# First operand tiles of the next stage split ahead of the last addition to x, state rows turned in other stages: a hybrid decoder step

## The chip, the cores and the metric

The kernel runs on one core of a Trainium2 chip. The metric is the device time of one execution in microseconds (us). TensorE does the matrix products (PE in the profile; PEld is its weight load), VectorE (DVE), ScalarE (ACT) and GpSimd (POOL) work on rows, and DMAs are issued by SyncE (SP) and by ScalarE. PSUM is the memory that TensorE writes, in eight banks of 512 floats for each of 128 partitions.

## The reference

One inference step of a trunk of two layers, for a prompt of 1024 tokens and for 8 single sample tokens with the same weights; D = 1024, F = 2816. Cut to what matters:

```python
for i in range(2):
    h = rmsnorm(x, norm_mix[i])
    # layer 0: pointwise + GLU, causal depthwise conv of width 31, LayerNorm, swish, pointwise (pw2)
    # layer 1: sliding-window attention, 16 heads over 4 kv heads, learned sinks, then w_o
    out = conv_module(h) if i == 0 else attention(h)
    x = x + out
    h = rmsnorm(x, norm_ffn[i])
    g, u = split(h @ ffn_w_in[i])              # 2 x 2816 columns
    x = x + (silu(dwconv3(g)) * u) @ ffn_w_down[i]
y = rmsnorm(x, norm_final)
# also returned: the last 30 rows of the GLU output, the last 128 keys and values,
# and the last two rows of each g, for the prompt and for the samples
```

## The kernel before

All 1032 tokens are the columns of x, which stays on the chip as 8 tiles X of 128 rows. A dense product is three matmuls per weight tile and chunk of 344 columns, since each operand is split into a rounded high part and the rest (weights by GpSimd, lines 577 and 579; operand tiles H by ScalarE, high part, and VectorE, rest). `dense` (line 1717) makes one output tile of 128 rows: 8 operand tiles k, 9 matmuls each, into banks 0 to 2 (side 0) or 3 to 5 (side 1), in turn. A norm's token scale is not applied to H. Only the norm's gain is; the sums of squares are turned into a scale while the next product already runs, and whoever takes the product multiplies by RS, the scale spread over all partitions.

The kernel meets four transitions, where a stage's last output is added to x and x becomes the next stage's operand: after pw2 (into the first ffn), after the first ffn (into qkv), after w_o (into the second ffn), and after the second ffn (into the end). At each of them `residual` runs on two engines. VectorE (line 854) adds a product to its X tile (`x_add`, lines 850 and 852), and sums squares that ScalarE made (`add_square`, line 819). ScalarE (line 1278) squares each X tile (line 1269). After the next-to-last tile, ScalarE waits until the last product is done (`s_mm`), since that product still reads H, and makes the high parts of H tiles 0 and 1 (line 1291); VectorE adds the last tile to x and makes the rest of tiles 0 and 1 (`split_lo`, line 812). Then ScalarE squares the last tile and makes high parts 2 to 7 in a loop (line 1296), and VectorE adds the last squares and makes the rests 2 to 7, in a loop too.

TensorE goes on with `dense(0, 0, wait_h=True, hooks={2: token_sums})`: it waits for each H tile, and after tile 2 it sums the squares over the partitions (`token_sums`, line 1776, 18 matmuls with one column each). ScalarE takes the roots (line 1274), VectorE the reciprocals (line 829), and in the second product, after tiles 1 and 4, TensorE spreads the scale (`broadcast`, line 1783, 16 matmuls; `broadcast_samples`, line 1790, 2). A hook stands in TensorE's instruction order, so a hook that waits holds up everything behind it.

In pw2 and w_o the eight products follow each other with 72 matmuls each. In the ffn, x is added to in passes of 8 groups of 18 matmuls (line 1762), which read MID and not H. The flag `wide` in VectorE's `residual` is for these: there it adds two tiles and then two squares.

Before pw2 stands the layer norm. ScalarE takes a root (line 1406), loads the table for Silu, and per tile makes a Silu and a copy into H (lines 1414 and 1416). TensorE meanwhile spreads scale and mean and then waits for H in `dense_pair` (line 1735).

The end, line 2052 of TensorE's program: `token_sums`; eight transposes of CKEEP (kept GLU rows); 44 of GKEEP (kept gate rows of both ffns, 10 rows per tile) in four parts of 11; then x, by 72 transposes of 128 columns. ScalarE first multiplies X by the last gain (line 1547), takes the roots between, and copies two of the four parts (line 1554); VectorE copies the others (lines 1234 and 1237). The y blocks are scaled by VectorE (even, line 1240) and ScalarE (odd, line 1558) and stored by SP (line 555), the sample row last (line 557). ScalarE's queue issues the six stores of kept rows after its last y block (lines 1561 to 1565). WK is a set of nine work tiles: 0 RS, 1 sum of squares, 2 and 3 squares, 4 to 6 the ffn's, 7 and 8 tables.

Of the kernel before, what the change touches and what calls it, by code (L numbers as in the profile page):

```python
# [126 lines left out]
def build(nc, a):  # L127
    ctx = ExitStack()
    with ctx:
# [135 lines left out]
        s_hh = sem("h_hi_ready")  # L265
        s_h = sem("h_ready")
# [68 lines left out]
        s_ka = sem("gate_rows_taken_by_act")  # L335
# [13 lines left out]
        GROWS = [WK[:, 6:9, :].rearrange("p a n -> p (a n)"), WK[:, 0:3, :].rearrange("p a n -> p (a n)")]  # L349
        HALF_F = F // 2  # L350

        def GATE_PS(part):

            return PS[0:2 + NS, 2 + 3 * part:5 + 3 * part, :].rearrange("p a n -> p (a n)")[:, 0:HALF_F]

        def Y_PS(b):

            pair = 2 * (b % 4)
            return PS[:, pair:pair + 2, :].rearrange("p a n -> p (a n)")
        LNOUT = [WK[:, k, 0:T] for k in (4, 5, 2)]  # L360
# [25 lines left out]
        STORES = 19  # L386
# [5 lines left out]
        def _(sp):  # L392
# [156 lines left out]
            yr.n = 5 + 3  # L549
# [7 lines left out]
            sp.dma_start(a["y_sample"][:, 0, :], WK[0:NS, 4, 0:D]).then_inc(s_st, 16)  # L557

            sp.wait_ge(s_st, 16 * STORES)

# [233 lines left out]
        def _(dve):  # L794
# [59 lines left out]
            def residual(side_of, bias, wide, row):  # L854
# [255 lines left out]
            def ffn(l):  # L1110
                norm_scale()
                base = l * NFR
                v.memset(GB[:, 0:2], 0.0).then_inc(s_v, own.up())
# [39 lines left out]
                with turns(dve, 0, FT // 4, dict([(mm, 24), (pr, 24), (own, 12)] + [(c, 4) for c in (t2, gc, silu, m_, mh, mid)])) as i:  # L1153
                    for o in range(2):
# [5 lines left out]
                        for m in range(1, KT):  # L1160
                            x_add(m, m % 2)
                residual(lambda o: o, None, True, R_MIX + 1 if l == 0 else None)
# [67 lines left out]

            token_scale()
            dve.wait_ge(s_rec, rec.at())
            dve.wait_ge(s_tr, tr.next())
            v.tensor_copy(WK[0:HIST + NS, 5, 0:D], PS[0:HIST + NS, 0:2, :].rearrange("p a n -> p (a n)")).then_inc(s_trr, trr.up())
            for l in range(2):
                dve.wait_ge(s_tr, tr.next(2))
                v.tensor_copy(GROWS[l][0:2 + NS, HALF_F:F], GATE_PS(1)).then_inc(s_trr, trr.up())  # L1237
# [5 lines left out]
            v.tensor_scalar(WK[0:NS, 4, 0:D], PS[0:NS, 0:2, :].rearrange("p a n -> p (a n)"),  # L1243
# [4 lines left out]
        def _(act):  # L1248
# [29 lines left out]
            def residual(row):  # L1278


                acc.n += 1
                with turns(act, 0, KT // 2 - 1, {pr: 2, acc: 2, sq: 2}) as i:
                    for o in range(2):
                        act.wait_ge(s_pr, pr.next())
                        square(tile(X, i * 2 + o), SQ[o])
                act.wait_ge(s_pr, pr.next())
                square(X[:, KT - 2, :], SQ[0])
                if row is not None:
                    act.wait_ge(s_mm, pr.n + 1)
                    for m in range(2):  # L1290
                        F_(H[:, 0, m, :], X[:, m, :], ACT.Identity, scale=par(m, row)).then_inc(s_hh, hh.up())
                act.wait_ge(s_pr, pr.next())
                square(X[:, KT - 1, :], SQ[1])
                if row is not None:
                    with turns(act, 2, KT, {hh: 1}) as m:
                        F_(htile(0, m), tile(X, m), ACT.Identity, scale=par(m, row)).then_inc(s_hh, hh.up())  # L1296
# [109 lines left out]
            F_(TOK[:, 1, :], TOK[:, 0, :], ACT.Sqrt, bias=EPSC[:, :]).then_inc(s_root, root.up())  # L1406
            cen = Count()
# [10 lines left out]
            residual(R_FFN)  # L1418
# [5 lines left out]
            def ffn(l):  # L1424
# [18 lines left out]
                value(0)  # L1443
                gate(1)
                value(1)
# [8 lines left out]
                residual(R_MIX + 1 if l == 0 else None)  # L1454
# [85 lines left out]
            residual(R_FFN + 1)  # L1540
# [3 lines left out]
            xg = Count()  # L1544
            act.wait_ge(s_acc, acc.at())
            for m in range(KT):
                F_(X[:, m, :], X[:, m, :], ACT.Identity, scale=par(m, R_FIN)).then_inc(s_xg, xg.up())  # L1547
                if m == KT // 2:
                    roots()
            turned, taken = 5, 5  # L1550
            ka = Count()
            for l in range(2):
                act.wait_ge(s_tr, turned + 2 + 2 * l)
                F_(GROWS[l][0:2 + NS, 0:HALF_F], GATE_PS(0), ACT.Copy).then_inc(s_ka, ka.up())  # L1554
            act.wait_ge(s_rec, sums.n + 1)
            for b in range(1, NB, 2):
                act.wait_ge(s_tr, turned + 6 + b)
                F_(YOUT[:, b, :], Y_PS(b), ACT.Identity, scale=TOK[:, 2, b:b + 1]).then_inc(s_ya, 1)
            act.wait_ge(s_ka, ka.at())
            act.wait_ge(s_trr, taken + 3)  # L1560
            act.dma_start(a["new_conv_prompt"][0, 0], WK[0:HIST, 5, 0:D]).then_inc(s_st, 16)
# [552 lines left out]
```

## Time and profile before

| | |
|---|---|
| median of 3 runs | 2465.25 us (2464.49 to 2466.59) |
| profiled execution | 2463.03 us |
| its span | 2461.2 us |
| mean granted clock of TensorE | 0.976 of full |
| busy, share of the span | PE 96%, PEld 93%, DVE 50%, POOL 32%, ACT 20% |

Times in the profile are us from the span's start. The line is that of the program printed above. [...] "<-" names what ended a wait.

### The profile page before, as it was taken

What the parts mean: (1) busy time and instruction counts of PE and PEld (TensorE: products, weight loads), DVE (VectorE), ACT (ScalarE), POOL (GpSimd) and SP (SyncE); (2) the same over time, 40 slices, a digit from 0 to 9 for tenths busy, and PEclk for the clock granted to TensorE, in tenths of its full rate; (3) what the DMA queues carried; (4) which work ended last, traced back from release to release, by engine and by line L of the source; (5) the groups of instructions that cost most, each with busy time, mean ns of one, the idle gap of its engine ahead of it and who ended that gap; (6) DMA issues with size and microseconds to landing.
All of it is one profiled execution on the core that took longest, in us unless ns stands there. A gap on an engine that the chain in (4) does not pass through costs nothing. (4 is left out here: it accounts for less than half of the span.)

```text
span 2461.2 us, 36800 instructions
## 1 busy us (share of the span) xinstructions
PE 2355.4 (96%) x15074; PEld 2300.1 (93%) x15074; DVE 1218.4 (50%) x1192; ACT 481.9 (20%) x776; POOL 780.6 (32%) x403
## 2 busy tenths in 40 slices
PE   7999978999999999999989899899999999999996
PEld 6999968899999999999989776889999999999996
DVE  4765565444444443444555698534444434434445
ACT  5111114210011110000120288221111100100014
POOL 2233422233333332333323244222333323323330
PEclk9999989999999999999989899999999999999998
DMA  7322331221211112111112110111121121121112
GB/s 210 74 68 68 83 129 26 60 79 43 52 43 48 46 43 51 43 47 47 43 36 63 23 52 1 35 43 43 44 52 44 43 52 43 44 52 44 51 36 75
DMA packets 175711, 134.09 MB, mean 54 GB/s; under 512 B 11185, under 2 KB 160449, under 8 KB 175263
## 3 DMA queue, kind: packets, MB, share of 16 engines
q1 hardware_dynamic: 168054, 121.78, 18.7%
q10 hardware_dynamic: 7549, 10.71, 1.6%
q8 instruction: 88, 1.44, 0.2%
q14 instruction: 20, 0.16, 0.0%
HBM read 109.42 MB, written 12.32 MB: 49 GB/s over the span
## 5 line engine op out<-in xcount | busy, mean ns | idle before, releaser
L1726 PE MATMUL PS<-H,W 128*128 128x344 f32 x9072 | 1455.9, 322 | 23.7 <-DVE H L812 17.7
L1726 PEld LDWEIGHTS PS<-H,W 128*128 128x128 f32 x9072 | 1444.5, 190 | 27.9 <-issue 17.2
L577 POOL CAST W<-RAW 128x1024 fp32r<-128x1024 f32 x176 | 205.7, 1169 | 1482.0 <-issue 753.4
L1762 PE MATMUL PS<-MID,W 128*128 128x344 f32 x3168 | 503.7, 320 | 1.4 <-DVE X L850 1.4
L1762 PEld LDWEIGHTS PS<-MID,W 128*128 128x128 f32 x3168 | 500.9, 188 | 1.7 <-DVE X L850 1.7
L579 POOL TENSOR_TENSOR W<-RAW,W 128x1024 fp32r<-128x1024 f32 x176 | 479.6, 2725 | 14.1
L850 DVE TENSOR_TENSOR X<-PS,X 128x1032 f32<-128x1032 f32 (+1 forms) x184 | 226.4, 1231 | 248.8 <-PE PS L1762 206.6
L1121 DVE TENSOR_TENSOR WK<-PS,WK 128x1032 f32<-128x1032 f32 x44 | 54.2, 1233 | 310.0 <-PE PS L1726 310.0
L1430 ACT ACTIVATE GKEEP<-WK 128x10 f32 (+1 forms) x44 | 9.3, 212 | 824.4 <-DVE WK L1121 824.4
L1141 DVE TENSOR_TENSOR WK<-PS,WK 128x1032 f32<-128x1032 f32 x44 | 54.2, 1232 | 183.3 <-PE PS L1726 181.0
L1928 PE MATMUL PS<-PB,EB 128*128 128x256 f32 x864 | 108.7, 288 | 13.2 <-issue 6.5
L1124 DVE SCALAR_TENSOR_TENSOR WK<-WK,FPAR 128x1024 f32<-128x1024 f32 x44 | 84.6, 1923 | 73.8 <-ACT WK L1431 73.8
L1928 PEld LDWEIGHTS PS<-PB,EB 128*128 128x128 f32 x864 | 107.5, 196 | 14.0 <-issue 6.7
L1147 DVE TENSOR_TENSOR MID<-WK,MID 128x1032 fp32r<-128x1032 f32 x44 | 88.5, 2010 | 27.3 <-ACT MID L1438 27.3
L1438 ACT ACTIVATE MID<-WK 128x1032 fp32r<-128x1032 f32 x44 | 47.1, 1070 | 246.4 <-DVE WK L1143 246.4
L624 POOL TENSOR_TENSOR PX<-PX,SMALL 128x1024 f32<-128x1024 f32 x32 | 60.6, 1894 | 103.1 <-DVE SMALL L688 103.1
L1433 ACT ACTIVATE WK<-WK 128x1032 f32<-128x1032 f32 x44 | 46.9, 1067 | 189.5 <-DVE WK L1132 189.5
L1269 ACT ACTIVATE WK<-X 128x1032 f32 (+1 forms) x32 | 34.1, 1066 | 192.8 <-DVE X L850 132.4
L819 DVE TENSOR_TENSOR WK<-WK 128x1032 f32<-128x1032 f32 x32 | 58.4, 1825 | 20.8 <-ACT WK L1269 20.5
L1639 PE MATMUL PS<-PT,VR 128*128 128x512 f32 x192 | 59.1, 427 | 2.7 <-ACT PT L1509 2.4
L1126 DVE SCALAR_TENSOR_TENSOR WK<-WK,FPAR 128x1024 f32<-128x1024 f32 x44 | 56.5, 1284 | 5.9 <-DVE WK L1124 0.2
L1501 ACT ACTIVATE PX<-PS,SMALL 128x256 f32<-128x256 f32 x128 | 58.7, 478 | 1.0 <-DVE SMALL L681 1.0
(213 smaller groups left out, 1495.8 us busy)
## 6 DMA issues: line engine op xcount, KB each, us to landing
RAW<-in_ffn_w_in SPq DMA_DIRECT2D x176, 256.0 KB, 3.8
RAW<-in_ffn_w_down SPq DMA_DIRECT2D x88, 256.0 KB, 3.7
RAW<-in_conv_w_pw SPq DMA_DIRECT2D x48, 256.0 KB, 4.1
PB<-GS SPq DMA_DIRECT2D x128, 64.0 KB, 2.0
RAW<-in_attn_w_qkv SPq DMA_DIRECT2D x24, 256.0 KB, 3.8
x_spill<-X SPq DMA_DIRECT2D x1, 4128.0 KB, 12.5
X<-x_spill SPq DMA_DIRECT2D x1, 4128.0 KB, 14.7
XIN<-in_x_prompt SPq DMA_DIRECT2D x8, 512.0 KB, 8.8
```

The costliest lines, as they stand in the source:

```text
L577: nc.gpsimd.tensor_copy(W[:, slot, 0, :], RAW[:, slot, :]).then_inc(s_hi, hi.up())
L579: nc.gpsimd.tensor_tensor(W[:, slot, 1, :], RAW[:, slot, :], W[:, slot, 0, :].bitcast(F32), ALU.subtract).then_inc(s_w, ready.up())
L624: nc.gpsimd.tensor_tensor(PX[:, b], PX[:, b], SMALL[:, b, 6, :].unsqueeze(2).broadcast_to((P, GROUP, 2 * P)), ALU.mult).then_inc(s_pn, 1)
L819: v.tensor_tensor(ACC, ACC, SQ[o], ALU.add).then_inc(s_acc, acc.up())
L850: v.tensor_tensor(x, side(s), x, ALU.add).then_inc(s_pr, pr.up())
L1124: v.scalar_tensor_tensor(t, GB[:, 1:1 + SEQ], fpar(f, base + FR_W + 1), t, ALU.mult, ALU.add).then_inc(s_v, own.up())
L1147: v.tensor_tensor(MID[:, q, 1, :], MM, MID[:, q, 0, :].bitcast(F32), ALU.subtract).then_inc(s_mid, mid.up())
L1501: F_(PX[:, b, g, :], PS[:, 2 * b + g // 2, (g % 2) * 256:(g % 2 + 1) * 256], ACT.Exp, scale=SCALE, bias=SMALL[:, b, 1, g:g + 1], accum_out ...
L1639: last = matmul(PS[:, 6 + b, :], vb[:, vp, :], PT[:, pp, s, :], start=(s == 0 and q == 0), stop=(s == 1 and q == 2))
L1726: last = matmul(PS[:, 3 * side + c, 0:CH], W[:, slot, wp, k * P:(k + 1) * P], H[:, hp, k, c * CH:(c + 1) * CH], start=(k == 0 and q == 0), ...
L1762: last = matmul(PS[:, 3 * side + c, 0:CH], W[:, slot, wp, t * BANK + m * P:t * BANK + (m + 1) * P], MID[:, first + t, hp, c * CH:(c + 1) * ...
L1928: last = matmul(PS[:, 6 + g % 2, (g // 2) * SPP:(g // 2 + 1) * SPP], EB[:, g % 2, wp, NPH * (NLAG - 1 - j):NPH * (NLAG - j), :].rearrange( ...
```

## The change

**Transitions.** FIRST = 3. VectorE makes the rests of H tiles 0 to 2 before the last `x_add`, the rests 3 to 7 after it, then the last squares; the loop is written out. ScalarE makes high parts 0 to 2 before the square of the next-to-last tile (after an ffn), or after it and after a new signal `s_hf` (after pw2 and w_o): TensorE gives it when the last product of the stage is through with operand tiles 0 to 2. High parts 3 to 6 follow when the last product is done, part 7 when the last x is there, and then its square. `token_sums` moves from tile 2 to tile 6 of the first product, the two broadcasts from 1 and 4 to 2 and 5 of the second.

**Kept rows.** CKEEP is turned before `dense_pair`, into banks 4 and 5; ScalarE copies it between its root and its first Silu; TensorE waits for that copy; SP stores it ahead of the later pw2 loads. The first ffn's gate rows are turned in the second ffn, in three parts, in the third and fourth product; ScalarE copies them after `value(0)` and `gate(1)` and issues their stores.

**End.** ScalarE multiplies each X tile by the last gain right after its square, with the table for the root loaded ahead. TensorE turns the second ffn's 22 gate tiles before `token_sums`; ScalarE copies 12, VectorE 10 of them; SP stores them ahead of y. The y blocks follow at once.

```diff
@@ SP
+            sp.wait_ge(s_ckt, 1)
+            sp.dma_start(a["new_conv_prompt"][0, 0], CROWS[0:HIST]).then_inc(s_cks, 16)
+            sp.dma_start(a["new_conv_sample"][0, :, HIST - 1, :], CROWS[HIST:HIST + NS]).then_inc(s_cks, 16)
...
+            sp.wait_ge(s_gkt, 4)
+            sp.wait_ge(s_gku, 1)
+            sp.dma_start(a["new_ffn_prompt"][1, 0], GROWS[1][0:2, 0:F]).then_inc(s_st, 16)
+            sp.dma_start(a["new_ffn_sample"][1, :, 1, :], GROWS[1][2:2 + NS, 0:F]).then_inc(s_st, 16)
@@ VectorE, residual
+                if row is not None:
+                    for m in range(FIRST):
+                        split_lo(m, X[:, m, :], par(m, row))
                 one(KT - 1)
                 if row is not None:
-                    for m in range(2):
+                    for m in range(FIRST, KT):
                         split_lo(m, X[:, m, :], par(m, row))
                 if wide:
                     add_square(0)
                 add_square(1)
                 acc_marks.append(acc.n)
-                if row is not None:
-                    with turns(dve, 2, KT, {hh: 1, h: 1}) as m:
-                        split_lo(m, tile(X, m), par(m, row))
@@ ScalarE, residual
+                if gain is not None:
+                    F_(TOK[:, 3, 0:1], EPSC[:, :], ACT.Sqrt)
...
                         square(tile(X, i * 2 + o), SQ[o])
+                        if gain is not None:
+                            gained(i * 2 + o, gain)
...
+                if row is not None and freed is None:
+                    first_sides(0, FIRST)
                 act.wait_ge(s_pr, pr.next())
                 square(X[:, KT - 2, :], SQ[0])
...
+                if freed is not None:
+                    act.wait_ge(s_hf, freed)
+                    first_sides(0, FIRST)
+                    act.wait_ge(s_mm, pr.n + 1)
                 if row is not None:
+                    first_sides(FIRST, KT - 1)
                 act.wait_ge(s_pr, pr.next())
+                if row is not None:
+                    first_sides(KT - 1, KT)
                 square(X[:, KT - 1, :], SQ[1])
@@ ScalarE, layer norm and second ffn
             F_(TOK[:, 1, :], TOK[:, 0, :], ACT.Sqrt, bias=EPSC[:, :]).then_inc(s_root, root.up())
+            act.wait_ge(s_ck, 1)
+            F_(CROWS, PS[0:HIST + NS, 4:6, :].rearrange("p a n -> p (a n)"), ACT.Copy).then_inc(s_ckt, 1)
...
                 gate(0)
                 value(0)
+                if l == 1:
+                    take_gate_rows(0)
+                    take_gate_rows(1)
                 gate(1)
+                if l == 1:
+                    take_gate_rows(2)
+                    act.wait_ge(s_gkt, 3)
+                    act.dma_start(a["new_ffn_prompt"][0, 0], GROWS[0][0:2, 0:F]).then_inc(s_gks, 16)
+                    act.dma_start(a["new_ffn_sample"][0, :, 1, :], GROWS[0][2:2 + NS, 0:F]).then_inc(s_gks, 16)
                 value(1)
@@ TensorE
+                    if free and k == FIRST - 1:
+                        last.then_inc(s_hf, 1)
...
+            for m in range(KT):
+                last = transpose(PS[0:HIST + NS, 4 + m // 4, (m % 4) * P:(m % 4 + 1) * P], CKEEP[:, m, :])
+            last.then_inc(s_ck, 1)
+            pe.wait_ge(s_ckt, 1)
             dense_pair()
...
+            def gate_rows(part):
+
+                if part == 0:
+                    pe.wait_ge(s_bcr, bcr.at())
+                else:
+                    pe.wait_ge(s_gkt, part)
+                for j, f in enumerate(range(8 * part, min(8 * part + 8, FT))):
+                    last = transpose(PS[0:2 + NS, 6 + j // 4, (j % 4) * P:(j % 4 + 1) * P], GKEEP[:, 0, f, :])
+                last.then_inc(s_gk, 1)
...
-                dense(0, 0, wait_h=True, hooks={2: token_sums})
-                dense(1, 1, hooks={1: broadcast, 4: broadcast_samples})
-                dense(0, 0)
-                dense(1, 1)
+                dense(0, 0, wait_h=True, hooks={6: token_sums})
+                dense(1, 1, hooks={2: broadcast, 5: broadcast_samples})
+                dense(0, 0, hooks=hooks[0])
+                dense(1, 1, hooks=hooks[1])
...
+            ffn(({1: lambda: gate_rows(0), 6: lambda: gate_rows(1)}, {3: lambda: gate_rows(2)}))
```

## Rows read from the trace of the kernel before

**Rows 1.** The page, parts 1 and 2: TensorE busy, granted clock in tenths
```profile
PE 2355.4 (96%) x15074; PEld 2300.1 (93%) x15074; DVE 1218.4 (50%) x1192; ACT 481.9 (20%) x776; POOL 780.6 (32%) x403
...
PEclk9999989999999999999989899999999999999998
```

**Rows 2.** Waits of TensorE, the whole span: total us, times, longest us
```profile
PE PS L1726 <- DVE H L812: 17.7, 6, 3.3
```

**Rows 3.** Windows: us, busy us of PE, PEld, DVE, ACT, POOL, PEclk, DMA
```profile
471.20:504.40 33.20, 27.17 (x154) 26.65 (x153) 16.46 (x12) 11.13 (x12) 8.04 (x4) 0.85 0.34 121
...
1238.00:1272.40 34.40, 28.71 (x153) 28.20 (x153) 18.35 (x14) 11.36 (x14) 7.87 (x4) 0.80 0.12 31
...
1652.60:1685.70 33.10, 27.10 (x155) 26.56 (x154) 16.44 (x12) 11.14 (x12) 8.03 (x4) 0.85 0.13 33
...
2421.60:2461.20 39.60, 19.12 (x142) 16.36 (x142) 14.67 (x12) 18.80 (x19) 0.00 (x0) 0.80 0.33 117
```

**Rows 4.** Timeline, first transition: start us, us, engine, line, work, [idle before]
```profile
473.89 3.06 PE L1726 MATMUL PS<-H,W 128*128 128x344 f32 x18 [2.68 <-DVE H L812]
...
474.31 6.38 ACT L1296 ACTIVATE H<-X,PAR  x6
...
476.86 9.41 DVE L812 SCALAR_TENSOR_TENSOR H<-X,PAR,H  x6
...
480.30 2.95 PE L1726 MATMUL PS<-H,W 128*128 128x344 f32 x9 [3.35 <-DVE H L812]
...
483.04 3.53 PE L1776 MATMUL PS<-CST,WK 128*128 128x1 f32 x18
...
504.14 0.38 PE L1790 MATMUL PS<-CST,TOK 8*128 8x8 f32 x2
```

**Rows 5.** Timelines: TensorE's prices at the full granted clock
```profile
2375.97 45.61 PE L1762 MATMUL PS<-MID,W 128*128 128x344 f32 x288
...
346.21 1.97 PE L1962 MATMUL PS<-CST,WK 128*128 128x1 f32 x18
...
497.99 1.95 PE L1783 MATMUL PS<-CST,TOK 128*128 128x128 f32 x16
```

**Rows 6.** Timeline, second transition: VectorE and GpSimd at the same time
```profile
1241.64 5.41 DVE L819 TENSOR_TENSOR WK<-WK 128x1032 f32<-128x1032 f32 x2
...
1242.70 3.25 POOL L579 TENSOR_TENSOR W<-RAW,W 128x1024 fp32r<-128x1024 f32 x1
```

**Rows 7.** Timeline, before pw2 (340 to 420): the layer norm's start
```profile
359.92 1.28 ACT L1414 ACT_TABLE_LOAD   x1
...
366.04 0.59 PE L1790 MATMUL PS<-CST,TOK 8*128 8x8 f32 x2 [1.32 <-DVE WK L840]
...
368.14 2.26 ACT L1414 ACTIVATE WK<-CONV,PAR 128x1032 f32<-128x1032 f32 x1 [6.94 <-DVE CONV L1091]
```

**Rows 8.** Timeline, the end (2370 to 2461)
```profile
2425.36 5.34 ACT L1547 ACTIVATE X<-X,PAR 128x1032 f32<-128x1032 f32 x5 [1.41 <-DVE WK L819]
...
2429.01 1.89 PE L1796 MATMUL PS<-CST,CKEEP 128*38 128x128 f32 x8
...
2430.72 1.28 ACT L1274 ACT_TABLE_LOAD   x1
...
2432.01 0.27 ACT L1274 ACTIVATE TOK<-PS,EPSC 128x8 f32<-128x8 f32 x1
...
2436.83 2.57 PE L1796 MATMUL PS<-CST,GKEEP 128*10 128x128 f32 x22 [2.94 <-ACT WK L1554]
...
2443.23 1.11 ACT L1558 ACTIVATE YOUT<-PS,TOK 128x1024 f32<-128x1024 f32 x1 [3.67 <-PE PS L1796]
...
2443.61 8.31 SPq L555 DMA_DIRECT2D out_y_prompt<-YOUT  x8
...
2451.96 1.56 SPq L557 DMA_DIRECT2D out_y_sample<-WK  x1
...
2453.96 1.48 ACTq L1565 DMA_DIRECT2D out_new_ffn_sample<-WK  x1
```

More of the change, by code:

```diff
@@ L348, in build @@
         acc_marks = []
[L349 to L354, printed above, removed]
+        GROWS = [WK[:, r:r + 3, :].rearrange("p a n -> p (a n)") for r in (1, 4)]
+        CROWS = WK[0:HIST + NS, 6, 0:D]
         def Y_PS(b):
@@ L1228, in _ @@
             ffn(1)
+            dve.wait_ge(s_gk, 5)
+            v.tensor_copy(GROWS[1][0:2 + NS, 12 * P:16 * P], PS[0:2 + NS, 7, :])
+            v.tensor_copy(GROWS[1][0:2 + NS, 16 * P:F], PS[0:2 + NS, 3:5, :].rearrange("p a n -> p (a n)")[:, 0:F - 16 * P]).then_inc(s_gku, 1)
             token_scale()
             dve.wait_ge(s_rec, rec.at())
[L1233 to L1237, printed above, removed]
             for b in range(0, NB, 2):
@@ L1715, in begin_group, with dense @@
                 pr.n += 1
-            def dense(side, slot, wait_h=False, hooks={}):
+            def dense(side, slot, wait_h=False, hooks={}, free=False):
                 pe.wait_ge(s_w, w.next())
@@ L2009, in _ @@
             ffn()
-            dense(0, 0, wait_h=True, hooks={2: token_sums})
-            dense(1, 1, hooks={1: broadcast, 4: broadcast_samples})
+            dense(0, 0, wait_h=True, hooks={6: token_sums})
+            dense(1, 1, hooks={2: broadcast, 5: broadcast_samples})
             dense(0, 0)
@@ L2047, in _ @@
                 dense(0, 0)
-                dense(1, 1)
-            ffn()
-            token_sums()
-            pe.wait_ge(s_pr, pr.at())
-            for m in range(KT):
-                last = transpose(PS[0:HIST + NS, m // 4, (m % 4) * P:(m % 4 + 1) * P], CKEEP[:, m, :])
-            last.then_inc(s_tr, tr.up())
-            trr.n += 1
-            for l in range(2):
-                for part in range(2):
-                    if l == 1 and part == 0:
-                        pe.wait_ge(s_ka, 1)
-                    if l == 1 and part == 1:
-                        pe.wait_ge(s_trr, trr.next())
-                    if l == 0 and part == 1:
-                        pe.wait_ge(s_root, sums.n + 1)
-                    for f in range(FT // 2):
-                        last = transpose(GATE_PS(part)[:, f * P:(f + 1) * P], GKEEP[:, l, part * FT // 2 + f, :])
-                    last.then_inc(s_tr, tr.up())
-            trr.n += 1
+                dense(1, 1, free=True)
+            ffn(({1: lambda: gate_rows(0), 6: lambda: gate_rows(1)}, {3: lambda: gate_rows(2)}))
+            pe.wait_ge(s_pr, pr.at(1))
+            for f in range(FT):
+                if f == 16:
+                    pe.wait_ge(s_pr, pr.at())
+                bank = 7 if 12 <= f < 16 else f // 4 if f < 12 else f // 4 - 1
+                last = transpose(PS[0:2 + NS, bank, (f % 4) * P:(f % 4 + 1) * P], GKEEP[:, 1, f, :])
+                if f == 11:
+                    last.then_inc(s_gk, 1)
+            last.then_inc(s_gk, 1)
+            token_sums()
             pe.wait_ge(s_xg, KT)
-            pe.wait_ge(s_ka, 2)
-            pe.wait_ge(s_trr, trr.at())
+            pe.wait_ge(s_gkt, 4)
             for b in range(NB):
+                if b == 1:
+                    pe.wait_ge(s_gku, 1)
+                if b == 3:
+                    pe.wait_ge(s_root, sums.n + 1)
                 if b >= 4 and b % 2 == 0:
```

83 lines of the change are left out of this document (47 added, 36 removed).

## The prediction

> **What bounds the kernel now.** I read the page first: TensorE is busy for 96% of the span, and its granted clock is full except in a few slices [rows 1]. So only time in which TensorE stands still or runs at half clock can be won, and it must be looked for in the dips. The waits of TensorE name one: six waits for the rest of an H tile, 17.7 us [rows 2]. That is three transitions with two waits each. The windows measure these transitions, from the end of a stage's last product to the end of `broadcast_samples` in the next one, and the end of the kernel [rows 3]. Each transition takes 33 to 34 us at a mean clock of 0.80 to 0.85; the end takes 39.6 us.
>
> The timeline shows where that goes in the first one [rows 4]: TensorE waits 2.68 us, does 18 matmuls of H tiles 0 and 1, waits 3.35 us because the rest of tile 2 stands behind the last addition, two rests and a square on VectorE, and then works at half clock: 9 matmuls take 2.95 us where a pass at full clock takes 45.61 us for 288, 0.158 each [rows 5]; `token_sums` takes 3.53 us where 18 such matmuls took 1.97 [rows 4, 5].
>
> **First and third transition (after pw2, after w_o).** The work in such a stretch is 117 dense matmuls (18 + 9 + 63 + 27), `token_sums` and the broadcasts. At full clock that is 117 x 0.158 = 18.5, plus 1.97, 1.95 and 0.38 [rows 4, 5]: 22.8 us. The stretches take 33.2 and 33.1 [rows 3], so 10.4 and 10.3 us are lost, 6.0 of each as waits and the rest to the clock. In the changed kernel three tiles are ready before the last product ends: `s_hf` comes with 45 matmuls (7.1 us) to go, and three high parts of 1.06 (6.38 for six [rows 4]) and one rest behind them end in about 4.6. TensorE then has 27 matmuls, 4.3 us, without a wait. In that time VectorE makes the last addition and the rest of tile 3. A rest costs about 1.25: six took 9.41 [rows 4], of which some 2 are a wait behind GpSimd. That wait is visible where two adds of VectorE took 5.41 us with a subtraction of GpSimd, 3.25, lying in them [rows 6]. GpSimd's pair starts with the first product of the stage, so it will meet the rests 3 to 7 now. VectorE needs 1.25 for the addition, 6 x 1.25 for five rests and a square, and 2.2 for the subtraction it meets, 11.0 us; TensorE reaches `token_sums` after 63 matmuls, 10.0 us. One wait of 1.0 us stays, and what is late next is that last square. **Gain: 9.4 and 9.3.** Bounds: 10.4 without any wait, 7.5 if GpSimd costs 2.9 instead of 2.2 and tile 4 is late too.
>
> **Second transition (after the first ffn).** It loses 34.4 - 22.8 = 11.6 us. Here all rests and squares crowd on VectorE: eight rests, the last addition and two squares, 11 x 1.25 = 13.8, plus 2.2 for GpSimd, less the one operation by which the first rest precedes the end of the last group: 14.7. TensorE's 63 matmuls take 10.0; 4.7 us of waits stay, in pieces of 2 or less. **Gain: 6.9.** Bounds: 11 and 2; at the lower one the clock falls as before, which costs 0.20 x 34.4 = 6.9 at most [rows 3].
>
> **End.** Now the last square is added at 2425.36, eight gains of 1.07 (5.34 for five) follow with a table load of 1.28 and the roots in their midst, then the kept rows, and the first y store is issued at 2443.61 [rows 8]. In the changed kernel a gain stands behind each square. Two squares and two gains (4.3) fit into two groups (36 x 0.158 = 5.7), but the last square waits for one gain: the sum is there at 2426.4. The 22 gate transposes (2.57) lie before that, under the squares. `token_sums` at 1.97 gives 2428.4 (3.53 at half clock is the other bound), roots and reciprocal 0.7; meanwhile eight transposes of y (2.57 x 8/22 = 0.9), then a scaling of about 1.2 (1.11 on ScalarE): first store at 2430.6. SP is moved two stores ahead of it, 1.5 each after the copies at about 2427.9, so it is free at 2430.9, and the two bounds meet. Eight issues of 8.31 and the sample's 1.56 end at 2440.6 [rows 8]. The landing of the sample row is not shown; from the last issue's end (2453.96 + 1.48) to the span's end lie 5.8 us, for rows nearly three times as long, so it is between 0 and 5.8, and I take 4. End at 2444.6: **gain 16.6.** Bounds: 18.5 (landing 2) and 12.5 (landing 5.8, sums at half clock, less one).
>
> **CKEEP before pw2.** The last broadcast ends at 366.63; eight transposes take 1.89, ScalarE's copy 1.11, and a table load 1.28 [rows 7, 8]. The load for Silu stood right behind the root, at 359.92, and was hidden in ScalarE's wait of 6.94 us [rows 7]; in program order the copy is now between, and the load follows the copy. The first Silu begins at 371.0 instead of 368.14. Silu and copy, 2.26 + 1.06 per tile, are more than TensorE's 18 matmuls (2.84), so ScalarE is the chain there and nothing takes the delay back. **Cost: 2.9.** Bounds: 0 (the load ahead of the copy after all, which would then lie in the old wait) and 3.5; less than nothing is excluded, as ScalarE's order only gains work. TensorE's own 1.89 lies in its wait for H. SP's wait for the copy delays no weight: the next pw2 loads need a RAW slot that frees only when `dense_pair` lets go of its weights.
>
> [...]
>
> **First ffn's gate rows in the second ffn.** 22 transposes on the bound engine, 2.57, that the end no longer pays but whose saving is already in its gain. The second part waits for ScalarE's copy of the first, behind `value(0)`: 0 to 1.1 (one copy [rows 8]), taken 0.4. **Cost: 3.0.** The copies and two store issues on ScalarE stand before `value(1)`, whose input needs the fourth product (72 matmuls, 11.4 us): hidden.
>
> **At nothing:** the broadcasts one tile later leave two tiles of product (2.8 us) for copying RS and taking the first product off side 0, two operations at 1.25; GpSimd starts its splits as early as the products that trigger them; the unrolled loops are the same operations.
>
> **Sum.** 9.4 + 9.3 + 6.9 + 16.6 - 2.9 - 3.0 = 36.3 us. The profiled execution took 2463.03, its span 2461.2; so 2426.7. The median of the runs shown, 2465.25, is 2.2 above it: **2429**.
>
> **Rivals.**
> *The clock falls again* in the second transition, where 4.7 us of waits lie within 15 us, and at the end, where TensorE has only transposes for 2.6 of 4.8 us. For: the full clock was lost in every transition [rows 3]. Against: in the first transition the clock stood through a wait of 2.68 (18 matmuls in 3.06 behind it) and fell at one of 3.35 [rows 4], while the new ones are 2 or less. Price 6.9 + 2: 2438. Chance 0.15.
> *The change doesn't do what it says:* ScalarE meets `s_hf` too late, because it stands behind the square of the next-to-last tile, and VectorE's rests come after the last addition as before. Then 2.68 comes back in the first and third transition: 2434. Against: 45 matmuls are left after the signal. Chance 0.08.
> *Slower:* the granted clock stays at half after a transition. Its place is the dense run behind the hooks, in which gate rows and broadcasts now break up the products; each us at half clock loses 0.5, so from 73 us of added half clock on, the gain is gone, and at 93 us the time is 2475. Against: before, 0.15 x 33.2 x 2 = 10 us at half clock in a transition, and then full clock on an unbroken run [rows 1, 3]. Chance 0.07, of which 0.03 for a length that lands within 0.2%.
>
> **Numbers.** The forecast has 0.70; its own range is 2421 (no CKEEP cost, landing 2, no late square) to 2434. With the falling clock and the late signal the range is 2421 to 2440. Faster by over 0.2% (5 us, about what a measurement can tell from no change): 0.70 + 0.15 + 0.08 = 0.93; same 0.03; slower 0.04.
>
> **What would show it.** Right: the six waits [rows 2] gone but for about 1 us twice and some 4.7 in the second transition; the stretches [rows 3] at clock 1.0 and near 24, 24 and 28 us; the first y store issued some 9 us behind the end of the last product, where it was 22 (2443.61 against 2421.6); a Silu table load behind a copy, and the first Silu 2.9 later. Wrong: a clock below 0.9 in two of the stretches, a wait for ScalarE's gate rows of more than 2 us, or a span that ends more than 26 us behind the last product.

## The result, and the profile after

The changed kernel takes **2435.62 us** (median of four runs, 2429.5 to 2437.24) against 2464.87 (four runs, 2461.21 to 2466.59): a ratio of **0.9879, 95% interval 0.9865 to 0.9892**. The forecast was 2429 in a range of 2421 to 2440. The profiled execution took 2434.49, its span is 2432.7, so 28.5 us less than the span of before, where the steps of the prediction add up to 36.3. The mechanism came out; 7.8 us of the gain did not come.

The page of the changed kernel, parts 1 and 2 (it answers to [rows 1]):

```profile
PE 2347.4 (96%) x15074; PEld 2290.4 (94%) x15074; DVE 1212.2 (50%) x1191; ACT 484.2 (20%) x780; POOL 782.5 (32%) x403
...
PEclk9999978999999999999999999999999999999999
```

The slices in which the granted clock dipped in the middle and at the end are at 90% or more now. One dip is left, a little deeper than before: the layer norm before pw2, in the sixth and seventh slices.

The windows of the changed kernel over the three transitions and the end (it answers to [rows 3]; columns: us, busy us of PE, PEld, DVE, ACT, POOL, then PEclk, DMA share, GB/s):

```profile
475.30:500.20 24.90, 24.40 (x163) 23.56 (x162) 12.04 (x9) 8.01 (x9) 7.83 (x4) 1.00 0.38 133
1238.50:1268.40 29.90, 26.45 (x164) 25.36 (x163) 16.32 (x14) 8.61 (x11) 8.09 (x4) 0.94 0.14 36
1647.10:1672.00 24.90, 24.38 (x163) 23.54 (x161) 12.05 (x9) 8.01 (x9) 7.83 (x4) 1.00 0.17 43
2410.20:2432.70 22.50, 14.26 (x114) 13.02 (x112) 11.68 (x11) 10.23 (x11) 0.00 (x0) 0.86 0.51 194
```

Each transition runs again from the end of a stage's last product to the end of `broadcast_samples`. That point now lies nine dense matmuls later in the program, 9 x 0.158 = 1.4 us, so the like-for-like lengths are 23.5, 28.5 and 23.5 against 33.2, 34.4 and 33.1. The clock is 1.00 in two of them and 0.94 in the one that keeps its waits; in e2 the first one has the same waits, 0.27 and 0.26 us, and 36 matmuls behind them take 7.46 us for 5.92, so the waits alone don't decide this (see why the prediction was right).

The timeline of the first transition in the changed kernel (it answers to [rows 4]; columns: start us, us, engine, line, work, and in brackets the idle time before and what ended it):

```profile
468.21 3.27 ACT L1307 ACTIVATE H<-X,PAR 128x1032 fp32r<-128x1032 f32 x3 [1.86 <-PE PS L1766]
469.41 3.70 DVE L825 SCALAR_TENSOR_TENSOR H<-X,PAR,H 128x1032 fp32r<-128x1032 f32 x3 [0.54 <-ACT H L1307]
...
475.33 1.29 DVE L865 SCALAR_TENSOR_TENSOR X<-PS,PAR,X 128x1032 f32<-128x1032 f32 x1 [2.21 <-PE PS L1766]
476.54 8.25 DVE L825 SCALAR_TENSOR_TENSOR H<-X,PAR,H 128x1032 fp32r<-128x1032 f32 x5
...
481.23 4.51 PE L1766 MATMUL PS<-H,W 128*128 128x344 f32 x27 [0.26 <-DVE H L825]
...
484.72 1.22 DVE L832 TENSOR_TENSOR WK<-WK 128x1032 f32<-128x1032 f32 x1
485.99 2.07 PE L1818 MATMUL PS<-CST,WK 128*128 128x1 f32 x18 [0.24 <-DVE WK L832]
```

Three tiles are split by 473.1, before VectorE makes the last addition at 475.33; TensorE goes from one stage into the next and waits 0.26 and 0.24 us in place of 2.68 and 3.35. The five other rests run in a row, 1.65 each with GpSimd's subtraction among them, and the last square ends at 485.94, the moment that TensorE wants it.

The timeline of the end in the changed kernel (it answers to [rows 8]):

```profile
2410.27 2.57 PE L1838 MATMUL PS<-CST,GKEEP 128*10 128x128 f32 x22
...
2413.23 1.23 DVE L832 TENSOR_TENSOR WK<-WK 128x1032 f32<-128x1032 f32 x1 [0.39 <-ACT WK L1284]
...
2414.52 2.23 PE L1818 MATMUL PS<-CST,WK 128*128 128x1 f32 x18 [1.69 <-DVE WK L832]
...
2420.07 7.99 SPq L566 DMA_DIRECT2D out_y_prompt<-YOUT  x8
...
2428.11 1.10 SPq L568 DMA_DIRECT2D out_y_sample<-WK  x1
```

The first y store is issued 9.9 us behind the end of the last product (2410.2), where it was 22; the gate rows turn under the last squares. The last issue ends at 2429.2, 3.5 us ahead of the span's end.

What the prediction does not have stands in the queues of the page (part 3: packets, MB, share of 16 engines) and in TensorE's timeline of the first ffn. The queue of instructions in the kernel before:

```profile
q8 instruction: 88, 1.44, 0.2%
```

TensorE's timeline there, at a turn of its loop:

```profile
781.59 22.92 PE L1762 MATMUL PS<-MID,W 128*128 128x344 f32 x144
804.35 45.60 PE L1726 MATMUL PS<-H,W 128*128 128x344 f32 x288
849.78 22.89 PE L1762 MATMUL PS<-MID,W 128*128 128x344 f32 x144
```

The queue of instructions in the changed kernel:

```profile
q8 instruction: 124, 2.03, 0.3%
```

and TensorE's timeline at the same turn:

```profile
777.49 22.91 PE L1804 MATMUL PS<-MID,W 128*128 128x344 f32 x144
801.66 45.72 PE L1766 MATMUL PS<-H,W 128*128 128x344 f32 x288 [1.27 <-DVE X L863]
847.23 22.89 PE L1804 MATMUL PS<-MID,W 128*128 128x344 f32 x144
```

Before, the products went on without a gap; now TensorE stands for 1.25 to 1.30 us at each of four turns (663.74, 801.66, 939.57, 1077.49), at one of them with no releaser but "issue", at the three others with an addition of VectorE for one, which at the same turns of before was never late. From the first to the last down product of the first ffn it is 667.2 us where it was 661.0. And 36 more packets of instructions are loaded, nine for each turn.

| step | predicted us | profiled execution |
|---|---|---|
| first, second, third transition | -9.4, -6.9, -9.3 | -9.7, -5.9, -9.6 |
| end | -16.6 | -17.1 |
| CKEEP ahead of the first Silu (square root to Silu) | +2.9 | +1.4 (8.54 to 9.91) |
| start of pw2's second group | - | -1.3 (the clock, 63 matmuls in 10 us for 55; see the last section) |
| gate rows in the second ffn | +3.0 | +3.2 |
| turns of the loop, first and second ffn | 0 | +6.2, +0.8 |
| layer norm's sums (square root at 363.71, was 359.60) | 0 | +4.1 |
| sum | -36.3 | -27.9 (span: -28.5) |

The right column sets one execution of each kernel against the other, and steps that the change does not touch differ by several us between kernels with the same code there (below).

### The profile page after: what moved, and what is told of

It reads as the page before. It is cut to its first block and busy times, and to the rows that moved or that the text cites. A ratio compares the mean times of both kernels' runs of the same rounds, so it can differ in the third digit from the quotient of the medians.

```text
span 2432.7 us, 36641 instructions
## 1 busy us (share of the span) xinstructions
PE 2347.4 (96%) x15074; PEld 2290.4 (94%) x15074; DVE 1212.2 (50%) x1191; ACT 484.2 (20%) x780; POOL 782.5 (32%) x403
```

## The experiments

All were compared with the kernel before on the same chip. Whether TensorE's turns have to do with where its code lies was asked first.

**The kernel before with its TensorE program moved by four instructions** (e1), and **the changed kernel with two SP loops written out** (e2; the first of the two is shown).

```diff
+            for _ in range(8):
+                pe.wait_ge(s_const, 16)
             pe.wait_ge(s_const, 16)
```
```diff
-            with turns(sp, 2, KT // 2, {ready: 2}) as i:
+            for i in range(2, KT // 2):
```

> The kernel before, with eight waits on a constant that is long there put ahead of TensorE's first instruction, where TensorE waits 11.7 us for x anyway; in the program that is four 64-byte instructions, so that TensorE's loop of the first ffn lies four instructions further on, as it does in the changed kernel (its last instruction goes from place 5630 to 5634; 16 KB are 256 instructions, and 22 x 256 = 5632). Theory (place of the code): the loop now reaches into an eighth block of 16 KB, its instructions are fetched again in every turn, and the four turns of the first ffn each lose 1.2 to 1.5 us that before did not: first ffn 5 to 6 us longer, the queue of instructions over 100 packets instead of 88, total 2469 to 2472 against 2464.9. Rival (the waits at the turns come from the new order of the transitions, or from additions that come later): nothing changes, 2465 within 2, the turns of the first ffn without a wait.

Measured: 2466.23 against 2464.38, ratio 1.0009 (1.0000 to 1.0019); 88 packets, no wait at a turn, 661.0 us. The page counts 36804 instructions for 36800. The rival's numbers.

> The changed kernel, with two of SP's loops of loads (last stage of the convolution block, and q of the attention) written out: the same DMAs in the same order, but four instructions fewer ahead of TensorE's first-ffn loop, which ends at place 5630 again as in the kernel before. Theory (place of the code): the four waits of 1.25 to 1.30 us at the turns of the first ffn (663.7, 801.7, 939.6, 1077.5) go, the first ffn is 5 to 6 us shorter, the queue of instructions back near 88 packets, total 2429 to 2431 against the changed kernel's 2435.6. Rival (the transitions' new timing makes them): waits stay, total 2435 within 3. The clock in the layer norm's sums decides another 0 to 6 us in either: read it from the stage apart.

Measured: 2436.73 against 2464.38, ratio 0.9890 (0.9875 to 0.9905); 124 packets, waits of 1.23 to 1.42 us at all four turns. Again the rival's numbers. But the two runs tell less than was meant, as both expectations have the change's shift of the loop wrong. Counted in the trace's records of TensorE, the turns of a loop once, the loop of the first ffn begins at 3767 in the kernel before, at 3771 in e1, and at 3783 in e2 as in the changed kernel. So e2 moved nothing, and e1 moved the loop by a quarter of what the change moves it: the change has exactly the 16 instructions of the eight CKEEP transposes more ahead of the loop (a weight load and a matmul each). The theory stood, with its place miscounted, and needed a proper test.

**The same padding with 16 instructions** (e5), on the kernel before:

> The kernel before with 32 waits on a constant that is long there ahead of TensorE's first instruction: 16 instructions in the program. Counted without the branch labels, which the first two runs suggest are not in the loaded program, TensorE's first-ffn loop begins at instruction 3800 in the kernels that did not fetch it again (before, the transitions alone; 3804 with the short padding) and at 3816 or 3817 in the three that did (the changed kernel, the SP loops written out, the conv rows late). Here it begins at 3816, with nothing of the change in it. Theory (place of the code): 120 to 125 packets of instructions instead of 88, all four turns of the first ffn wait 1.2 to 1.4 us, the stretch from its first to its last down product is 667 instead of 661.0, total 2470 to 2472. Rival (something of the change itself makes TensorE wait at the turns): 88 packets, 661.0, 2464 to 2467.

Measured: **2472.66** against 2464.82, ratio 1.0038 (1.0026 to 1.0051). The queue of instructions in this kernel, which has nothing of the change but the shift:

```profile
q8 instruction: 124, 2.03, 0.3%
```

and TensorE's timeline at the turn of before:

```profile
785.52 22.91 PE L1762 MATMUL PS<-MID,W 128*128 128x344 f32 x144
809.56 45.70 PE L1726 MATMUL PS<-H,W 128*128 128x344 f32 x288 [1.13 <-issue]
855.10 22.89 PE L1762 MATMUL PS<-MID,W 128*128 128x344 f32 x144
```

Waits of 1.10 to 1.45 at all four turns, 667.0 us; the page counts 36816 instructions for 36800. The place of the code alone makes the loss; the new order of the transitions is not needed for it. The loop of the first ffn begins at 3800 or 3804 in the five kernels with 88 packets and at 3816 or 3817 in the six with 124; the twelfth is the next one. These are counts in the compiled program; those of TensorE's records in the traces are 33 less in every kernel (3767, 3771, 3783, 3784; of e7 and e8, within 2), so the distances are the same.

**Both loops put where they fit** (e6): the conv rows late (below), the first gate-row copy ahead of `value(0)` (TensorE's wait for it is 0.69 us in the changed kernel), and fillers, one instruction between two products, 236 of them in the first groups of pw1 and pw2 and 104 in q. With them the loops of the two ffns begin 3 and 4 instructions ahead of the place that the first has in the kernel before, whole packets of 256 instructions (last section) left out:

```diff
+                            pad()
...
+            def pad():
+                if pads[0] > 0:
+                    pads[0] -= 1
+                    pe.wait_ge(s_const, 16)
+                    pe.wait_ge(s_const, 16)
```

> [...] Theory (place of the code): no wait at any of the eight turns; first ffn 661.0 instead of 667.2, second 660.5 to 661 instead of 664; with the wait of 0.69 about 10 us less than the 2435.4 of the conv rows late: 2425 to 2427, packets of instructions about 55. [...] Rival 2 (the second ffn's turns wait for something else): its stretch stays at 663 to 664, total 2429 to 2430.

Measured: **2423.29** (2422.08 to 2428.11), ratio **0.9841 (0.9828 to 0.9855)**: 12.3 us under the changed kernel, and the fastest version of this study. Its queue of instructions:

```profile
q8 instruction: 53, 0.87, 0.2%
```

and TensorE's timeline at one turn of the first and one of the second ffn:

```profile
772.51 22.92 PE L1816 MATMUL PS<-MID,W 128*128 128x344 f32 x144
795.27 45.60 PE L1767 MATMUL PS<-H,W 128*128 128x344 f32 x288
...
1941.84 22.92 PE L1816 MATMUL PS<-MID,W 128*128 128x344 f32 x144
1964.60 45.60 PE L1767 MATMUL PS<-H,W 128*128 128x344 f32 x288
```

No wait at any of the eight turns: the first ffn 661.0 again, the second 659.3, where before had 663.3 and the changed kernel 664.1. The second loop had been loaded anew in every turn in the kernel before too, unseen, at 0.69 to 0.77 us each, as here:

```profile
1987.48 45.72 PE L1726 MATMUL PS<-H,W 128*128 128x344 f32 x288 [0.77 <-issue]
```

The 340 fillers cost nothing that shows: from the `broadcast_samples` ahead of pw2 to the first down product, with 140 of them between, it is 202.7 us in e6 and in e4, and from the one of qkv to the second ffn's first down product, with the 104 of q between, 477.3 us for 480.9.

**The transitions alone**, on the kernel before (e3; the diff is the change's, without the state rows and the end):

> The kernel before with the three transitions of the change alone (first three operand tiles split ahead of the last addition, the release of the first tiles, token sums after the seventh tile's products, broadcasts one tile later); state rows and the end as before. By the prediction's terms: 9.4 + 6.9 + 9.3 = 25.6 less, 2439; by what the changed kernel's profile showed for them, 9.8 + 6.0 + 9.6 = 25.4. TensorE's first-ffn loop ends at place 5618 here, so by the theory of the code's place nothing is lost at its turns: 2439 to 2440. Rival (the turns' waits come from the transitions): 6 us of it given back, 2445 to 2446. The layer norm's sums: if their half clock in the changed kernel's profile was chance, they stand here as before (square root of the variances at 359.6 within 1) as often as not.

Measured: 2442.69 (2437.16 to 2445.11) against 2464.38, ratio 0.9904 (0.9891 to 0.9918): 21.7 less. 88 packets, 661.0 in the first ffn: nothing lost at its turns, as the place of the code has it. The gain is some 4 us short of the terms; in this profile, which is of the slowest of the five runs, the second ffn's turns took 1.0 more than before, the end 2.3 more (41.9 for 39.6), and the 45 us around the first transition were at a clock of 0.96.

Which half of it brings the gain, the split ahead or the order on TensorE? **The changed kernel with the early order** (e7), **the order alone** (e9) and **the split alone** (e10), the last two on the kernel before:

```diff
-                dense(0, 0, wait_h=True, hooks={2: token_sums})
-                dense(1, 1, hooks={1: broadcast, 4: broadcast_samples})
+                dense(0, 0, wait_h=True, hooks={6: token_sums})
+                dense(1, 1, hooks={2: broadcast, 5: broadcast_samples})
```
(e9 is this, twice; e7 is its reverse on the changed kernel; e10 is e3 without it.)

> The changed kernel with the token sums after the third tile's products again and the broadcasts after the second and the fifth, as in the kernel before, the split ahead kept. Theory of the prediction (the sums behind the products hide the last square): TensorE now stands after 27 products for the last square, which ends at 485.9 in the changed kernel's profile while the 27 products end near 480.5: a wait of 4.5 to 5.5 us in the first and the third transition, 5 to 6 in the second, with a clock that may fall behind it for another 0 to 5 us each; 14 to 20 us in all, 2450 to 2456. Rival (with the split ahead, the splits of the later tiles hold TensorE anyway, so that the wait only moves): under 4 us in all, 2436 to 2439.

Measured: 2456.16 (2444.71 to 2460.73), ratio 0.9959 (0.9938 to 0.9980), 20.5 over the changed kernel: the prediction's mechanism, at the upper end. TensorE's timeline in the first transition:

```profile
483.06 3.70 PE L1818 MATMUL PS<-CST,WK 128*128 128x1 f32 x18 [6.43 <-DVE WK L832]
486.69 12.54 PE L1766 MATMUL PS<-H,W 128*128 128x344 f32 x63
```

One wait of 6.43 us for the last square (8.93 in the second transition), longer than expected, and the clock falls behind it: the sums at 3.70 instead of 2.07, 63 matmuls in 12.54 instead of 10.0.

> The kernel before with the order on TensorE alone changed (token sums behind the seventh tile's products, broadcasts one tile later), the splits where they were. Theory A (from the early hooks in the changed kernel, which cost 20 us: nearly all of the transitions' gain is the order on TensorE, and the split ahead only feeds it): in the first transition the splits of tiles 3 to 8 end at 486.3 in the profile of before, so seven tiles of products end near 486.2, where the changed kernel has 486.0, with waits for tiles of 2.7 and 3.4 us in pieces: 2443 to 2447, within 4 of the 2442.7 of both together. Theory B (both are needed, as the prediction's terms have it: the first tiles' late split takes 2 to 4 us of each transition and the clock falls in those waits): 2450 to 2458.

Measured: 2460.23 against 2463.16, ratio 0.9987 (0.9979 to 0.9996). Theory A, formed from e7, falls; B had 2450 or more and is nearer, but too kind as well.

> The kernel before with the splits ahead and the early release alone, token sums after the third tile's products and the broadcasts after the second and fifth, as before. Theory A (the order on TensorE carries the gain): TensorE stands for the last square after 27 products as before, only longer in one piece (6.4, 8.9 and 6.4 us in the changed kernel with early hooks, against 17.7 in all before): 2460 to 2467, no gain that can be told from none. Theory B (each half brings its share): 2452 to 2458.

Measured: 2465.08 against 2463.16, ratio 1.0005 (0.9996 to 1.0014): no gain, as A had it for this half, and no loss that can be told from none. TensorE's waits over the whole span (total us, times, longest), of e9:

```profile
PE PS L1726 <- DVE H L812: 19.2, 6, 4.5
```

and of e10:

```profile
PE PS L1787 <- DVE WK L821: 25.6, 4, 8.9
```

The kernel before waited 17.7 us for tiles [rows 2]. With the order alone TensorE waits for the same tiles, 19.2; with the split alone it has the tiles and waits for the sums' last square, 25.6 (the fourth wait is the end's). Each half alone trades one wait for another and keeps the fall of the clock (0.90 in the three stretches of e9, 0.77 to 0.82 in those of e10, 0.80 to 0.85 before); both together take 21.7 us. They don't add: a gain of 2.9 and no gain make no 21.7.

**The first tiles released late** (e8):

```diff
-                    act.wait_ge(s_hf, freed)
-                    first_sides(0, FIRST)
                     act.wait_ge(s_mm, pr.n + 1)
+                    first_sides(0, FIRST)
```

> The changed kernel with the first operand tiles released only by the end of the last product of pw2 and of w_o, as before, instead of after that group's third tile; DVE's order (three splits ahead of the last addition) kept. Theory of the prediction (the early release carries the first splits under the last products): ScalarE begins the first side at the products' end, DVE splits three tiles (3.7 us and a first side of 1.07 ahead) before it adds the last tile, the last addition and with it square and sums come 4 to 5 us later, in two transitions: 8 to 11 us, 2444 to 2447. Rival (the first splits are hidden by what follows, the last square sets the end in either): under 3 us, 2435 to 2439.

Measured: 2440.56 (2435.84 to 2448.99), ratio 0.9909 (0.9887 to 0.9930): 4.9 over the changed kernel, between the two expectations, but its four runs lie 13 us apart. The stretches themselves tell more. TensorE waits for H tiles again, in the first transition 2.67 and then 0.60 us, in the third 2.66 and 1.66, and the sums come late:

```profile
473.91 5.87 PE L1765 MATMUL PS<-H,W 128*128 128x344 f32 x27 [2.67 <-DVE H L825]
...
486.35 2.07 PE L1817 MATMUL PS<-CST,WK 128*128 128x1 f32 x18
...
1661.95 2.07 PE L1817 MATMUL PS<-CST,WK 128*128 128x1 f32 x18
```

The last products end at 471.2 and 1646.9, so the sums begin 15.1 us behind them in both, where it is 10.7 in the changed kernel: 4.4 later each, the theory's 4 to 5. VectorE adds the last tile at 476.87, behind three rests. To the end of `broadcast_samples` the two stretches take 29.4 and 30.9 us for 24.9 and 24.9, at a granted clock of 0.94 for 1.00: 10.5 us in all, inside the expected 8 to 11. That the profiled executions, 2440.52 and 2434.49, differ by 6.0 only is due to other stages; the square root ahead of pw2 alone came 4.2 us earlier (359.54 for 363.71). The 5.4 at which the prediction had put a late `s_hf` is the first wait, twice 2.7, and too little.

**The conv rows late** (e4):

```diff
-            F_(CROWS, PS[0:HIST + NS, 4:6, :].rearrange("p a n -> p (a n)"), ACT.Copy).then_inc(s_ckt, 1)
...
             h.n = 2 * KT
+            act.wait_ge(s_ck, 1)
+            F_(CROWS, PS[0:HIST + NS, 6:8, :].rearrange("p a n -> p (a n)"), ACT.Copy).then_inc(s_ckt, 1)
```

> The changed kernel with the convolution rows turned into banks 6 and 7 behind the broadcast, and copied and stored by ScalarE behind the layer norm's last tile in place of ahead of its first Silu; the place of TensorE's loop stays past the border (5635). Theory (the copy and the table load behind it stand on the path of the layer norm): the stretch from the square root to the first Silu goes from 9.91 back to 8.5 to 8.6, total 1.3 to 1.5 less than the changed kernel (2434), the turns of the first ffn still at 1.25 to 1.30. Rival (the transposes or the copy make the next stage's start late wherever they are): the stretch keeps 1 us or the second pair of products of the next stage starts later by as much.

Measured: 2435.39, ratio 0.9884 (0.9869 to 0.9899): the stretch from the root to the Silu goes to 8.34 (10.18 in e2, 9.91 in the changed kernel), and the total does not move by more than the runs differ. The transposes go to banks 6 and 7 here and the two stores to ScalarE, which the diff leaves out. Where the 1.8 us went, the windows of the 10 us from the start of pw2's second group show, in e2 (copy ahead of the Silu):

```profile
403.80:413.80 10.00, 9.91 (x63) 9.92 (x64) 4.19 (x3) 1.07 (x1) 3.66 (x2) 1.00 0.44 107
```

and in e4:

```profile
402.40:412.40 10.00, 9.92 (x53) 9.93 (x54) 4.17 (x3) 1.06 (x1) 3.65 (x2) 0.83 0.42 107
```

e4 begins the group 1.4 us earlier, at a clock of 0.83, and does ten matmuls fewer in 10 us, which is 1.6 us. Neither theory had that.

## Why the prediction was right, and where it was wrong

**Transitions: right in mechanism; the size (25.2 for 25.6) is in part luck.** The waits left are 0.26 and 0.24 in the first, 0.27 and 0.25 in the third, where 1.0 each was predicted, and 0.36, 0.31 (of the weight load), 1.66 and 1.39 in the second, 3.7 where 4.7 was predicted "in pieces of 2 or less". The late last square was named as what is late next, and in the second transition it is (1.39 for `token_sums`). In the second transition the clock is 0.94, between the forecast and the rival in which it falls: 5.9 for 6.9. The argument against that rival was that the clock stands through waits of 2 or less. The 36 matmuls behind `token_sums` show that it need not; the first line is of the first transition of the changed kernel, the next three of its second, the last of the first transition of e2:

```profile
487.99 5.92 PE L1766 MATMUL PS<-H,W 128*128 128x344 f32 x36
...
1245.32 5.91 PE L1766 MATMUL PS<-H,W 128*128 128x344 f32 x36 [1.66 <-DVE H L825]
...
1252.63 2.07 PE L1818 MATMUL PS<-CST,WK 128*128 128x1 f32 x18 [1.39 <-DVE WK L832]
...
1254.63 7.46 PE L1766 MATMUL PS<-H,W 128*128 128x344 f32 x36
...
485.05 7.46 PE L1766 MATMUL PS<-H,W 128*128 128x344 f32 x36
```

In e2, e3, e4 and e6 the first transition has waits of 0.25 to 0.27, as here, and yet these 36 take 7.28 to 7.48 us, some 1.5 more than in the changed kernel; why the clock falls in one execution and not in the other is open. The prediction treated split and order as one step; e9 and e10 show that this was necessary, as no part of it can be priced by itself. The two together, without the rest of the change, measured 21.7 (e3).

**End: right** (17.1 for 16.6). The sums took 2.23, nearer to the full clock's price than to the half clock's 3.53, and the first store came 9.9 behind the last product for the 9 predicted. The landing, taken as 4, was 3.5. Of the "two bounds" that were said to meet, one was misread: the two stores ahead of y were issued in 0.26 and 0.27 us and not 1.5 each, so SP was free long before, and the scaling of the first block (done at 2420.04) set the start.

**CKEEP: the mechanism right, the size wrong.** The table load moved behind the copy, as predicted:

```profile
363.71 0.30 ACT L1439 ACTIVATE TOK<-TOK,EPSC 128x9 f32<-128x9 f32 x1 [11.99 <-DVE TOK L1087]
...
370.21 1.05 PE L1838 MATMUL PS<-CST,CKEEP 128*38 128x128 f32 x8
...
371.30 1.02 ACT L1441 ACTIVATE WK<-PS 38x1024 f32<-38x1024 f32 x1 [7.28 <-PE PS L1838]
372.33 1.28 ACT L1449 ACT_TABLE_LOAD   x1
...
373.62 2.25 ACT L1449 ACTIVATE WK<-CONV,PAR 128x1032 f32<-128x1032 f32 x1
```

The term that was mis-sized is the eight transposes: 1.89 in [rows 8] was a price at half clock (granted 0.50 there), 1.05 is what they took. That is 0.8 of the 1.5 us that were missing; another 0.5 is the last broadcast, which ended 6.6 behind the root where it was 7.0, at a higher clock and not by the change. Against e4, whose broadcasts took what those of e2 took, the copy's cost in this stretch is 1.8 (10.18 for 8.34). And the step "nothing takes the delay back" failed: behind it pw2's second group ran at the full clock, which gave 1.6 of that back (e4).

In the same rows the load starts at the copy's end and the Silu at the load's, 372.33 + 1.28.

**Gate rows: right** (3.2 for 3.0): 1.04, 1.04 and 0.82 for the transposes, each overlapping the next product by some 0.2, and one wait of 0.69 for ScalarE's copy, inside the bounds of 0 to 1.1. e6 took that wait away by placing the copy ahead of `value(0)`.

**The step that failed is "At nothing: ... the unrolled loops are the same operations".** It counts operations, and no term has the place of TensorE's code. The 16 instructions of the CKEEP transposes, whose own time does lie in TensorE's wait for H, push the loop of the first ffn, 1768 instructions long, to a place from which it is loaded anew in every turn: 6.2 us in a stage that the change never touches. e5 shows it on the kernel before, e6 by removing it. The 0.8 in the second ffn did not come with it: e1, e3, e9 and e10, at 88 packets, take 664.0 to 664.4 there, so the 663.3 of the kernel before was a short one. With 6.2 in the sum the forecast of 2429 would have been 2435. That 2435.6 was measured is in part luck, as what is left of the misses has both signs (+4.1 and +0.8 that are no part of the change, -1.5 at CKEEP, -1.3 in pw2).

**By chance, and not by the change:** in the changed kernel's profiled execution the layer norm's sums ran at half clock (a granted clock of 0.50 between 350 and 363.7), and the square root came 4.1 us later than in the kernel before. The last sums of this stage in the changed kernel, in e2 and in the kernel before:

```profile
359.80 3.54 PE L2004 MATMUL PS<-CST,WK 128*128 128x1 f32 x18
...
356.59 3.54 PE L2004 MATMUL PS<-CST,WK 128*128 128x1 f32 x18
...
357.26 1.97 PE L1962 MATMUL PS<-CST,WK 128*128 128x1 f32 x18
```

They took 3.54 in ten of the twelve profiled executions, and 1.97 only in those of the kernel before and of e6; so the half clock is the usual case, and the kernel before was lucky in the execution that the prediction was read from. The rest of the spread is where the sums begin, at 342.2 to 346.2. In e2, e7 and e8, which share the changed kernel's code up to there, the root came at 360.5, 360.5 and 359.5; in e9, where the code up to there is that of before, at 365.5. The same kernel's runs differ by 8 us (2429.5 to 2437.24), of which this can be a part.

**The rivals:** the clock did not stay at half, and `s_hf` came in time (ScalarE's first sides start at 468.21, seven us ahead of the last product's end).

## What to carry to other kernels

Count the instructions of a long loop on TensorE (1768 here), and look at the instruction queue's packets before and after a change: when they rise, as here from 88 to 124, the loop may have come to lie badly, and instructions added anywhere ahead of it (16 here) can be the cause. When two things hold one engine at a hand-over (its tiles and its sums), price a change that removes only one of them at nothing: here one brought 2.9 us and the other nothing, and both 21.7. And a microsecond of delay can be free, or a microsecond saved can be lost: e4 took 1.8 us off the way to the first Silu, and 1.6 of them went at a granted clock of 0.83, where e2 had 1.00.

## What the runs showed of the hardware

**TensorE's loop and its code.** The queue's packets are 16 KB (36 more for 0.59 MB). In the kernel before, eight of them come between 485.2 and 646.1 us, 131 KB, while TensorE starts 2027 matmuls and weight loads: some 64 bytes for an instruction and 256 instructions in a packet, an estimate from these figures. A turn of the loop has 1768 instructions in every trace (864 matmuls, 864 weight loads and 40 others), 6.9 packets by that estimate. Where the first ffn's loop begins at 3800 or 3804 (before, e1), 4 packets come between 577 and 1190 us; where it begins at 3816 (the changed kernel, e5), 39 come, some nine more for each of the four turns, and the turn waits 1.0 to 1.7 us (all six kernels with 124 packets). Counted from the last multiple of 256, the loops that stay begin at 212 to 220 (e6's two at 213 and 212), the first ffn's that do not at 232 or 233. The border lies between; it was not narrowed. The theory of an eighth block, in e1's expectation, is not shown: counted from the program's first instruction every one of these loops would touch eight, and where the blocks begin no run shows. A loop of 6.9 packets can go back to its start without a wait: in e6, with 4 packets between 577 and 1190 us and 2 between 1780 and 2360.

**The clock behind one and the same wait.** At the start of pw2's second group TensorE waits 2.5 us for GpSimd's split in all twelve kernels. In the four that have ScalarE's copy ahead of the first Silu (the changed kernel, e2, e7, e8) the next 10 us are at a granted clock of 1.00, with 63 matmuls; in the eight others (before, e1, e3 to e6, e9, e10) at 0.83 to 0.85, with 53 to 55. In the 22 us that end with this wait the clock is 0.99 or 1.00 in all of them, and TensorE is busy for 19.0 of them in the four and 19.2 to 19.3 in the eight, which is too little to tell them apart by. What does is open: the copy starts the whole group of products 1.4 to 1.8 us later against what came before it, and no run tried that delay without the copy.
